# Between the layers of a two-block network: residual adds issued early, their transposes later, and one copy moved ahead of the logarithms

## The reference, cut to what matters

```python
x = x + rms_norm(f, norm_ffn_post[l])          # end of the first block
...
for l in range(DEPTH_2):                        # two layers
    h = rmsnorm(x, pre_norm_g[l])
    z = h @ w_in[l]
    ...
    mem_n = rmsnorm(mem, mem_norm_g[l])
    mv = (mem_n @ w_mv)                         # needs nothing of x
    ...
    x = x + rmsnorm(o, post_norm_g[l])          # end of each layer
...
log_a = jax.nn.log_sigmoid(g_lr @ w_gate_up[l] + b_gate[l]) / GLA_GATE_TAU
```

## Time and profile before

| | |
|---|---|
| median of 3 runs | 2390.75 us (2390.04 to 2391.03) |
| the profiled execution | 2387.95 us |
| its span in the profile | 2386.2 us |
| TensorE busy, share of the span | 2357.2 us, 99% |
| DVE busy | 1322.9 us, 55% |
| ACT busy | 1172.0 us, 49% |
| POOL busy | 28.0 us, 1% |
| mean share of the DMA engines | about 60% |

### The profile page before, as it was taken

How to read it: one execution, slowest core, us unless ns; L and a number is a source line. 1 busy time by engine, 2 the same in 40 slices (tenths; PEclk the granted TensorE clock), 3 DMA queues, 4 the chain that set the end, 5 groups by cost and what they waited for, 6 DMA issues and landing times.

```text
span 2386.2 us, 27602 instructions
## 1 busy us (share of the span) xinstructions
PE 2357.2 (99%) x11143; PEld 1962.6 (82%) x11143; DVE 1322.9 (55%) x1713; ACT 1172.0 (49%) x1543; POOL 28.0 (1%) x36
## 2 busy tenths in 40 slices
PE   9999999999999999999999999989999998999997
PEld 7788888888888888888888888878888887888886
DVE  6554455555557654454445555675555655555554
ACT  5445544444445644444444444465555455565443
POOL 0000000000000000000000000000000000000000
PEclk9999999999999999999999999999999999999999
DMA  8555555666667566665666566655555664655553
GB/s 296 150 159 168 159 148 148 199 201 193 197 203 266 183 186 187 192 190 186 196 188 193 189 191 207 222 164 180 154 166 160 205 209 133 198 159 154 164 194 119
DMA packets 237887, 438.87 MB, mean 184 GB/s; under 512 B 16816, under 2 KB 43056, under 8 KB 237120
## 3 DMA queue, kind: packets, MB, share of 16 engines
q1 hardware_dynamic: 237328, 436.90, 59.9%
q10 hardware_dynamic: 432, 0.20, 0.0%
HBM read 434.96 MB, written 2.10 MB: 183 GB/s over the span
## 4 chain that ended last, share of the span: by engine, by line
PE 82%; issue 14%; DVE 2%; ACT 1%; DMA 0%; SPq 0%; POOL 0%; DVEq 0%; ACTq 0%; POOLq 0%
PE pm L957 25%; PE pm L959 25%; PE pm L958 25%; PE pb L570 2%; PE pb L671 1%; DVE X L1481 1%; DVE wl L1947 1%; PE pb L795 0%; ACT wh L1405 0%; DMA raw<-in_w_in 0%; PE pb L649 0%; PE pb L648 0%; PE pb L611 0%; DVE xT3l L1432 0%; PE pb L624 0%
## 5 line engine op out<-in xcount | busy, mean ns | idle before, releaser
L1947 DVE TENSOR_TENSOR wl<-raw,wh 128x1024 fp32r<-128x1024 f32 (+3 forms) x787 | 949.6, 1209 | 931.9 <-ACT wh L1405 931.4
L1405 ACT ACTIVATE wh<-raw 128x1024 fp32r<-128x1024 f32 (+3 forms) x787 | 821.6, 1046 | 995.9 <-PE pm L959 992.5
L957 PE MATMUL pm<-wh,hTh 128*128 128x512 f32 x702 | 279.5, 398 | 0.5 <-DVE wl L1947 0.4
L957 PE MATMUL pm<-wh,x2Th 128*128 128x512 f32 x704 | 275.3, 391 | 0.0
L959 PE MATMUL pm<-wh,x2Tl 128*128 128x512 f32 x704 | 274.1, 389 | 0.0
L958 PE MATMUL pm<-wl,x2Th 128*128 128x512 f32 x704 | 274.0, 389 | 0.0
L959 PE MATMUL pm<-wh,hTl 128*128 128x512 f32 x702 | 273.6, 390 | 0.0
L958 PE MATMUL pm<-wl,hTh 128*128 128x512 f32 x702 | 273.3, 389 | 0.0
L957 PE MATMUL pm<-wh,xT3h 128*128 128x512 f32 (+1 forms) x640 | 251.4, 393 | 0.0
L959 PE MATMUL pm<-wh,xT3l 128*128 128x512 f32 (+1 forms) x640 | 245.0, 383 | 0.0
L958 PE MATMUL pm<-wl,xT3h 128*128 128x512 f32 (+1 forms) x640 | 244.5, 382 | 0.0
(11 more groups left out here) (377 smaller groups left out, 3106.4 us busy)
## 6 DMA issues: line engine op xcount, KB each, us to landing
raw<-in_w_in SPq DMA_DIRECT2D x286, 512.0 KB, 3.7
raw<-in_w_ffn_gate SPq DMA_DIRECT2D x88, 512.0 KB, 4.1
raw<-in_w_ffn_up SPq DMA_DIRECT2D x88, 512.0 KB, 3.7
raw<-in_w_ffn_down SPq DMA_DIRECT2D x88, 512.0 KB, 4.1
raw<-in_w_o SPq DMA_DIRECT2D x64, 512.0 KB, 3.9
raw<-in_w_in SPq DMA_DIRECT2D x68, 256.0 KB, 3.1
raw<-in_w_branch_b SPq DMA_DIRECT2D x32, 512.0 KB, 3.6
raw<-in_w_out SPq DMA_DIRECT2D x32, 512.0 KB, 4.6
```

Source lines behind the costliest of these rows:

```text
L957: e.matmul(o, ah[:, kk, t], h[:, c], start=first, stop=False)
L1405: e.activation(h[:, 0:n], r[:, 0:n], ACT.Copy).then_inc(s["hi"], 1)
L1947: e.tensor_tensor(l[:, 0:n], r[:, 0:n], h[:, 0:n].bitcast(F32), ALU.subtract).then_inc(s["lo"], 1)
```

## The change

Three things change, all in the order of instructions; no instruction is added or removed.

- The four adds of a residual are due at F + 4, F + 6, F + 8 and F + 11, instead of F + 4, F + 8, F + 12 and F + 16. Only the last is yielded behind a low part, low 0; before, each was yielded behind the low parts of the quarters before it.
- Turn i is due at F + 9 + 2i instead of F + 6 + 2i, high i and low i one step after it, and the variance at F + 28 instead of F + 24. The two transposes of the memory keys behind them (second layer) and their copies are due three steps later too. On ACT the covering group's accumulator is taken between high 2 and high 3; before, it was between high 4 and high 5.
- On ACT `qk0` is taken out ahead of the load of the logarithms' table and of the logarithms, due at step 68 instead of 69.

```diff
+ADDS, TURNS = (4, 6, 8, 11), 9
...
     def mk_turns(l):
         for i in range(2):
-            yield p.end[f"mk{l}"] + (2, 6)[l] + 2 * i
+            yield p.end[f"mk{l}"] + (2, 9)[l] + 2 * i
...
-            yield from residual_turns(l + 1, [p.first[BETWEEN[l]] + 6 + 2 * i for i in range(8)])
+            yield from residual_turns(l + 1, [p.first[BETWEEN[l]] + TURNS + 2 * i for i in range(8)])
...
         for i in range(8):
-            yield p.first[BETWEEN[l]] + 7 + 2 * i
+            yield p.first[BETWEEN[l]] + TURNS + 1 + 2 * i
             residual_high(r, i, 6 + i % 2, f"pre{l}", "fu10" if l == 0 else "gb0_")
             if i % 2:
                 residual_squares(r, i // 2, 8 * r + 2 + 2 * (i // 2))
-            if i == 4:
+            if i == 2:
                 yield L
                 taken(0, BETWEEN[l], m.MST[1] if l else m.mv[1], scale="mem")
         if l:
             for i in range(2):
-                yield L + 7 + 2 * i
+                yield L + 10 + 2 * i
...
-        yield DECAY[3] + 4
-        for i in range(4):
-            w.wait_ge(s["la_a"], i + 1)
-            e.activation(m.latmp[:, i, :], m.latmp[:, i, :], ACT.Ln, bias=1.0).then_inc(s["la_a"], 1)
         for h in range(4):
-            yield p.end[f"qk{h}"] if h else QK0 - 3
+            yield p.end[f"qk{h}"] if h else QK0 - 4
             if h >= 2:
                 w.wait_ge(s["qk_t"], 2 * h - 2)
             taken(0, f"qk{h}", m.ring[h % 2], scale="x")
+            if h == 0:
+                yield DECAY[3] + 4
+                for i in range(4):
+                    w.wait_ge(s["la_a"], i + 1)
+                    e.activation(m.latmp[:, i, :], m.latmp[:, i, :], ACT.Ln, bias=1.0).then_inc(s["la_a"], 1)
...
     def residual(l, tag, src, before):
 
         r, F = l + 1, p.first[BETWEEN[l]]
-        for i in range(8):
-            if i % 2 == 0:
-                yield F + 4 + 2 * i
-                w.wait_ge(s["rstd"], RS[tag])
-                w.wait_ge(s[before[0]], before[1])
-                if i == 6:
-                    w.wait_ge(s["scl"], SC[tag])
-                add(r, tag, src, part(i // 2))
-            yield F + 7 + 2 * i
+        for c in range(4):
+            if c == 3:
+                yield F + TURNS + 1
+                low_x(r, 0, f"pre{l}")
+            yield F + ADDS[c]
+            w.wait_ge(s["rstd"], RS[tag])
+            w.wait_ge(s[before[0]], before[1])
+            if c == 3:
+                w.wait_ge(s["scl"], SC[tag])
+            add(r, tag, src, part(c))
+        for i in range(1, 8):
+            yield F + TURNS + 1 + 2 * i
             low_x(r, i, f"pre{l}")
-        yield F + 24
+        yield F + 28
         variance(f"r{r}", DM, SQ[f"r{r}"])
```

## The result

| | before | after |
|---|---|---|
| median, us | 2390.39 (2388.03 to 2391.03, 4 runs) | 2372.97 (2372.90 to 2373.30, 4 runs) |
| the profiled execution, us | 2387.95 | 2373.30 |
| its span, us | 2386.2 | 2371.5 |

The changed kernel is faster: ratio 0.9929, with a 95% interval of 0.9912 to 0.9946. The profiled executions lie 14.65 us apart, against a forecast of 15.05. Two things therefore have to be explained: what went as forecast, and where 2.4 us more came from. The run of before that joined the three of the prediction took 2388.03 us, near the profiled execution; the other three lie 2.0 to 3.0 us above it.

The account below looks back on a forecast made before the run. TensorE was taken to bound the kernel, stalled mainly by transposes of X waiting for adds. Residuals 14.46 + queries 0.59 = 15.05 us off the median 2390.75 gave 2375.7 us; range 2374.0 to 2381.0, the forecast's own 2374.5 to 2377.

Parts of the forecast that it names:

- The sum: Whole kernel: stalls removed in the residuals, 14.46 us, and at the queries, 0.59 us, make 15.05 us.
- Residuals: Both residuals: TensorE's stalls at the transposes of X all go, 7.76 and 6.70 us, 14.46 together.
- Queries: First transpose of stg: its wait for ACT's copy, behind table load and logarithms, goes; 0.59 us.
- the walk: First residual, new order carried through each engine: add 0 stays slow, later adds take 1.4 us, turns find inputs ready.
- the one tight place: ACT at the covering group's end, F + 16: work queues behind it, leaving low 4 0.9 us before turn 6.
- Each later quarter repeats the pattern: Residuals before: later adds, like add 1, stand behind low parts and a waiting wl on DVE while TensorE stands.
- so no clock is won or lost: TensorE in the profiled stretch: granted clock 1.00 although it idled 7 of 39 us, so no clock effect.
- I take the difference off the median: Final step: 15.05 us off the median 2390.75, not the profiled 2387.95, giving 2375.7 us.
- A: Rival at turn 6: it comes too early for its bank, waiting 1 to 2.6 us per residual; 2378 to 2380.9; chance 0.12.
- B: Rival at the residuals: TensorE waits for wl instead of adds; as now less 0.6, 2390.2 us; chance 0.05.
- C: Rival at the banks' loop: turns 2 to 7 wait in each residual, so slower, up to 2406.9 us; chance 0.03.
- D: Rival at the residuals: only one of the two gains; 2382.4 to 2383.5 us; chance 0.03.

Follow-up runs that it names:

- experiments 2 and 3: 2: changed kernel run again, no edit, 2373.02 us; 3: changed kernel without the edit at the queries (residual edits alone), 2373.75 us.
- experiment 5: Kernel before, with one ACT edit: covering group taken out behind high 6 instead of high 4; 2386.10 us, ratio 0.9985.
- experiments 1 and 4: 1: kernel before run again, no edit, 2389.70 us; 4: kernel before with only the edit at the queries, 2389.04 us.
- experiments 5 and 6: 6: kernel before with six extra matmuls, results unused, just ahead of turn 6 of each residual; 2388.39 us, ratio 0.9993.
- experiment 7: Changed kernel with each add again behind the low parts of the quarters before it, later turns and early take kept; 2383.95 us, ratio 0.9976.
- experiment 8: Changed kernel with the turns back at F + 6 + 2i, early adds and early take kept; 2388.06 us, ratio 0.9993.

## Why the prediction was wrong

**The sum was right.** Residuals forecast at 14.46 us, measured 7.79 + 6.73 = 14.52. Queries forecast at 0.59, measured 0.59 by the rows and 0.73 by the medians of experiments 2 and 3. Add 0, beside POOL's multiply, was slow again and the moved adds were not, as the walk had it. The walk through the new order met the turns to 0.1 us (1585.2 and 1585.16; 1604.3 and 1604.38) and found the one tight place. One reading of the trace of before fell short without harm to the sum: "Each later quarter repeats the pattern" leaves out why turn 6 waited 2.56 us and turns 2 and 4 only 1.5. The other 1.1 us came from taking out the covering group ahead of it on ACT (experiment 5).

**The step that failed is the one on the clock**: "so no clock is won or lost". A loss of clock was put at nothing from one stretch of one execution, and in that execution neither residual had a fall. In others the granted clock went to 0.50 at turn 6, at 1.4 to 1.6 us a time; that was shown by the traces of experiments 1 and 4, and its cause by experiments 5 and 6. The changed kernel has no such stretch and saves those too. That is how the sum came to be taken off the wrong number: "I take the difference off the median" took stalls measured in an execution without falls off a median that holds them. 2387.95 - 15.05 = 2372.9 was the forecast for an execution without falls, and the changed kernel, which has none, took 2372.90 to 2373.30. The warning was in the first table: the profiled execution lay 2.1 us below the shortest of the three runs. It should have been a term with its own bounds: one or two falls of 1.4 to 1.6 us taken off the 2375.7 give 2372.5 to 2374.3, and the measured 2372.97 lies inside.

The Trainium skill (TensorE: Matmul & The Clock Gate, section "Part 1: The HAM clock gate") says that a hardware block sets the clock by how busy TensorE has been of late. The traces agree in kind: idle stretches of 2.56 and 3.0 us were followed by falls in some executions, and those of 1.53 us and less between the layers in no trace.

**The rivals.** A, B and C did not come: TensorE waits neither for low parts nor, behind the start, for `wl`. Nor did D: both residuals gained. Experiments 7 and 8 show that A's fear had a ground, though in other orders: with the take ahead of high 3 and either half missing, a turn waits 3.0 us.

**What stays open.** Why the same idle stretch, of 2.56 us or of 3.0, is followed by a fall in one place or execution and not in the next was not tried. An experiment with the same long wait at a step that is shifted against the rest would be the way.

## What to carry to other kernels

Where the profiled execution and the median differ by more than the runs among themselves, find out what differs before taking a difference off either. A stall of the bounding engine can cost more than its own length, as the clock may fall behind it; here the longest one was worth removing first (experiment 5), and the spread of the executions told whether the clock had fallen. In an in-order queue, issue an operation where its inputs are ready and not where it belongs in the program's text, and check for each wait on the bounding engine's own progress what stands behind it.

## What the runs showed of the hardware

- Behind TensorE's idle stretch of 2.56 us the granted clock fell to 0.50 in some executions and stayed at 1.00 in others; a fall cost 1.39 and 1.58 us. Behind 3.00 us of idle time in experiment 8, turn 6 came 6.03 us after turn 5 instead of 3.2; behind 3.05 us in experiment 7 the clock stayed at 1.00.
- Six matmuls whose results nobody reads, 1.52 us in a wait of 2.56, took the falls away and cost at most 0.4 us (2388.39 against the shortest execution of before, 2388.02).
- Beside POOL's multiply, add 0 on DVE took 2.43 us for two halves before the change and 2.44 after it, instead of 1.40. At the second residual of before, where the multiply had ended by 1979.50 and add 0 began at 1980.51, it took 1.40. No run moved POOL's multiply.
